# A hybrid decoder step on one core: input projection as seven block products, output projection from float16 parts

## The chip, the cores and the metric

The kernel runs on one core of a Trainium2 chip. The metric is device time in microseconds (us); lower is better. Each core has TensorE (PE, with its weight loads as PEld), VectorE (DVE), ScalarE (ACT), GpSimd (POOL) and SyncE (SP, which here only issues DMAs). Every engine runs its own instructions in program order and waits on semaphores for the others.

## What is computed

Two layers run over 2048 prompt tokens and 64 sample tokens (8 sequences of 8), with a model width of 1024.

```python
h = rmsnorm(x, norm_pre)
p = h @ w_in          # 1024 x 3344, cut into four head groups
# A short gated convolution    (x, b, c, z: 256 columns each)
# B gated linear attention     (q, k, v, z: 256 each, and 16 columns of a low-rank gate)
# C sliding-window attention   (q 256, k 128, v 128, z 256)
# D attention to 256 memory tokens (q, z: 256 each)
x = x + rmsnorm(concat(A, B, C, D) @ w_out, norm_post)
```

All of it is float32. The states and caches of the groups are outputs too.

## The kernel before, in words

The program is a sequence of stages: `start` (norm and transposes of the first 1024 tokens, and the products of the memory tokens), then four passes: layer 0 tokens 0 to 1023, layer 0 tokens 1024 to 2047 with the 64 sample tokens, and the same for layer 1. Each pass is a stage `units` (input projection and head groups) and a stage `out` (output projection, norm, residual, and the transposed h of the next pass).

A float32 product is made of float16 parts. h and the weights are scaled and split into a high and a low part, and a product is high x high, low x high and high x low: three "pieces". h lies transposed in `h_hi` and `h_lo`, 8 blocks of 128 rows (k) by tokens. The input weights are cut into 26 tiles of 128 columns and a narrow one of 16 (the gate, `lr`). For each tile and each step of 512 tokens (in the second passes also spans that take in the sample tokens, of 320 and 256 columns) PE runs 8 k x 3 pieces into one of two PSUM banks that alternate:

```python
        def proj_bank(it):
            return it["inst"] % 2
```

An instance waits until the reader of the one before the last has freed its bank. ACT reads most tiles out of PSUM (L2308, L2304), DVE some of group A (L2511, L2514). Weight tiles live in a ring of four (`w_raw` float32, `w_parts` high and low). In a first pass SP loads them (L1765), POOL scales them in place (L2841), ACT makes the high part (L2281), POOL the low one (L2836), and SP keeps both in DRAM (L1773), from where the second pass loads them (L1759).

Eight units (D0, B0, B1, C0, A0, C1, D1, A1: head group and half) follow each other in a pass. The order of everything in a pass, on all engines, comes from `plan_units`, which lays pieces of projection between the rows of the units' own work by estimated durations. So a wait of one engine holds all that stands behind it.

The output projection (L3011) takes the mixed heads and `w_out` in float32r high and low parts, again three pieces of 8 k, 512 columns each, two halves of the width: 48 matmuls a tile of 128 tokens. It waits for the bank's reader two turns back. In `start`, POOL's only steps in the loop over 8 token tiles are `mean ** -0.5` (the rows of L1283, called pow here), DVE's norm of a tile waits for its pow, and PE transposes the tile.

## Time and profile before

| what | value |
|---|---|
| timed runs, median | 2183.58 us (2179.11, 2183.58, 2184.03) |
| profiled execution | 2180.1 us span, 3.5 us below that median |
| PE busy | 2071.0 us, 95% |
| DVE busy | 1228.0 us, 56% |
| ACT busy | 855.0 us, 39% |
| POOL busy | 335.2 us, 15% |
| unit stages | 48 to 453, 553 to 1015, 1112 to 1525, 1622 to 2074 us |

Busy is the time in which an engine executes; shares are of the span. Matmuls are pipelined, so a busy PE need not be PE at its peak. The time between the stages named is the start and the four output stages.

### The profile page before, as it was taken

The page shows a single profiled execution, that of the slowest core. Times are in us where ns is not written, and L with a number is a line of the kernel's source. Part 1 is how long each engine was busy: PE and PEld are TensorE (multiplying, and loading weights), DVE is VectorE, ACT ScalarE, POOL GpSimd, SP SyncE. Part 2 cuts the span into 40 slices and gives each one's busy share as a digit, 9 for nine tenths or more (in the row PEclk, how much of TensorE's full clock was granted, in tenths as well). Part 3 has the DMA queues.
Part 4 walks back from the last instruction along what each step waited for, and adds up shares of the span by engine and source line. Part 5 has one row for each costly group of instructions (what it writes and reads, how often), then busy time and mean ns, then how long its engine had stood idle before and what let it go on. Part 6 is the DMA issues. An engine that isn't in the chain of part 4 may idle for free. (4 is left out here: it accounts for less than half of the span.)

```text
span 2180.1 us, 43454 instructions
## 1 busy us (share of the span) xinstructions
PE 2071.0 (95%) x16698; PEld 1321.2 (61%) x16698; DVE 1228.0 (56%) x2763; ACT 855.0 (39%) x1981; POOL 335.2 (15%) x267
## 2 busy tenths in 40 slices
PE   8999899999999998997999998999999999999898
PEld 4555455568666665666855444455776666656677
DVE  5477665455367754553645775555644776644423
ACT  4554333444354332333435542343435453232311
POOL 1443332000000000000133342320100000000000
PEclk9999999999999999998999998999999999999999
DMA  7431223347410222335353132223561113131532
GB/s 263 128 98 50 75 72 97 97 154 257 118 48 24 65 61 69 85 101 193 127 137 105 62 84 82 83 89 108 188 237 49 60 41 82 35 94 42 159 123 87
DMA packets 196936, 224.92 MB, mean 103 GB/s; under 512 B 53974, under 2 KB 138460, under 8 KB 196700
## 3 DMA queue, kind: packets, MB, share of 16 engines
q1 hardware_dynamic: 193620, 211.55, 31.3%
q10 hardware_dynamic: 3112, 10.59, 1.5%
q8 instruction: 135, 2.21, 0.4%
q14 instruction: 69, 0.57, 0.1%
HBM read 144.98 MB, written 66.10 MB: 97 GB/s over the span
## 5 line engine op out<-in xcount | busy, mean ns | idle before, releaser
L1934 PE MATMUL bank<-h_hi,w_parts 128*128 128x512 f16 (+4 forms) x4240 | 841.1, 344 | 17.5 <-ACTq L2309 9.8
L1934 PEld LDWEIGHTS bank<-h_hi,w_parts 128*128 128x128 f16 (+1 forms) x4240 | 403.2, 98 | 360.4 <-issue 58.0
L1934 PE MATMUL bank<-h_lo,w_parts 128*128 128x512 f16 (+3 forms) x2160 | 441.3, 343 | 3.4 <-DVEq L2560 1.1
L1934 PEld LDWEIGHTS bank<-h_lo,w_parts 128*128 128x128 f16 (+1 forms) x2160 | 205.4, 98 | 176.6 <-issue 18.9
L3011 PE MATMUL bank<-scr_r,tb_r 128*128 128x512 f32 x768 | 192.3, 409 | 21.5 <-DMA scr_r<-w_out_kept 12.4
L3011 PEld LDWEIGHTS bank<-scr_r,tb_r 128*128 128x128 f32 x768 | 149.4, 197 | 56.0 <-issue 13.0
L2308 ACT ACTIVATE tb<-bank 128x512 f32<-128x512 f32 (+1 forms) x140 | 71.3, 509 | 247.8 <-PE bank L1934 227.4
L2841 POOL TENSOR_SCALAR w_raw<-w_raw 128x1024 f32<-128x1024 f32 x46 | 129.6, 2822 | 80.0 <-DMA w_raw<-in_w_in 79.6
L3078 ACT ACTIVATE junk<-bank 128x512 bf16<-128x512 f32 (+1 forms) x68 | 40.6, 597 | 243.7 <-PE bank L3011 233.4
L2441 ACT ACTIVATE scr<-bank,stat 128x256 f32<-128x256 f32 x256 | 117.4, 470 | 34.0 <-DVE stat L2787 31.2
L2461 ACT ACTIVATE scr<-bank 128x1024 f32<-128x1024 f32 x64 | 65.5, 1023 | 163.7 <-PE bank L2205 163.3
L3011 PE MATMUL bank<-w_hi,tb_r 128*128 128x512 f32 x512 | 128.5, 395 | 0.7 <-DVEq L3159 0.7
L2836 POOL TENSOR_TENSOR w_parts<-w_raw,w_parts 128x1024 f16<-128x1024 f32 x46 | 103.5, 2252 | 165.8 <-ACT w_parts L2281 165.6
L2645 DVE COPY_PREDICATED scr<-level_mask,bank 128x128 f32<-128x128 uint8 (+1 forms) x332 | 116.8, 352 | 11.3
L3011 PEld LDWEIGHTS bank<-w_hi,tb_r 128*128 128x128 f32 x512 | 95.5, 188 | 22.3 <-DVEq L3159 1.2
L2304 ACT ACTIVATE tb<-bank 128x512 f32<-128x512 f32 (+1 forms) x80 | 40.7, 508 | 148.9 <-PE bank L1934 116.0
L2857 POOL TENSOR_TENSOR stat_g<-stat_g,minus_half 128x8 f32<-128x8 f32 (+1 forms) x20 | 29.2, 1462 | 403.5 <-DVE stat_g L2693 403.5
L2801 DVE TENSOR_SCALAR scr<-scr,stat 128x256 f32<-128x256 f32 x264 | 87.5, 393 | 2.5
L2810 DVE TENSOR_TENSOR mix_t<-bank,tb 128x256 f32<-128x256 f32 x64 | 27.1, 424 | 95.6 <-PE bank L2230 94.3
L2546 DVE SCALAR_TENSOR_TENSOR tb<-tb,gate_raw 128x512 f32<-128x512 f32 (+1 forms) x80 | 47.6, 594 | 46.2 <-ACT gate_raw L2305 44.2
L2205 PE MATMUL bank<-ident,scr 128*128 128x128 f32 x512 | 69.4, 278 | 3.6 <-DVE scr L2801 3.3
L2774 DVE SCALAR_TENSOR_TENSOR bank<-bank,win_mask 128x512 f32<-128x512 f32 x64 | 44.8, 699 | 43.6 <-PE bank L2186 40.2
(304 smaller groups left out, 2813.8 us busy)
## 6 DMA issues: line engine op xcount, KB each, us to landing
w_in_kept<-w_parts SPq DMA_DIRECT2D x104, 256.0 KB, 4.3
w_parts<-w_in_kept SPq DMA_DIRECT2D x104, 256.0 KB, 2.9
w_raw<-in_w_in SPq DMA_DIRECT2D x48, 512.0 KB, 4.1
out<-scr SPq DMA_DIRECT2D x32, 512.0 KB, 2.6
scr<-in_x_prompt SPq DMA_DIRECT2D x16, 512.0 KB, 4.3
w_out_kept<-scr_r SPq DMA_DIRECT2D x16, 512.0 KB, 6.3
scr_r<-w_out_kept SPq DMA_DIRECT2D x16, 512.0 KB, 5.9
scr<-out SPq DMA_DIRECT2D x16, 512.0 KB, 4.2
```

What stands on the lines that cost most here:

```text
L1934: m = mm(bank[b][0:m_w, 0:c1 - c0], w[:, k, 0:m_w], h[:, k, c0:c1], start=it["piece"] == 0 and k == 0, stop=it["piece"] == 2 and k == KT - 1)
L2205: m = nc.tensor.transpose(bank[b][:, (2 * h + i) * P:(2 * h + i + 1) * P], p[:, o:o + P], ident[:])
L2308: fn(part_of(s, role, pt), src, ACT.Copy, scale=scale).then_inc(tile_copied, 1)
L2441: m = fn(p[:, 256 * x:256 * x + 256], bank[6 + h][:, 256 * i:256 * i + 256], ACT.Exp, bias=z[:, 4 + x:5 + x], scale=1.0 if unit == "C" els ...
L2461: fn(pt.rearrange("p (b n) -> p b n", b=2), psum[:, 2:4, :], ACT.Copy).then_inc(bank_free[2], 1)
L2546: link(stt(z, z, 1.0, raw_gate(span, pt), ALU.add, ALU.mult))
L2645: m = nc.vector.copy_predicated(a.rearrange("p h (m i r) -> p h m i r", i=2, r=v)[:, :, :, 1, :], mask.to_broadcast([w, 2, w // (2 * v), v ...
L2774: link(stt(at[i], at[i], scale, mask.to_broadcast([P, 2, 256]), ALU.mult, ALU.add))
L2801: m = ts(p[:, n * h:n * h + n], p[:, n * h:n * h + n], z[:, at_inv + h:at_inv + h + 1], None, ALU.mult)
L2836: tt(lo_of(t), w_raw[:, t % RING, :, 0:split_width(t)], hi_of(t), ALU.subtract).then_inc(w_lo_done, 1)
L2841: nc.gpsimd.tensor_scalar(raw, raw, W_UP, None, ALU.mult).then_inc(w_scaled, 1)
L3011: m = nc.tensor.matmul(bank[b].rearrange("p (j n) -> p j n", j=RING), lhs[:, t % 2, k, :], rhs[:, :, k, :], start=j == 0 and k == 0, stop= ...
```

## The change

**Input projection.** Tokens, k and weight columns are each cut in two halves: a step's 512 tokens into 256 and 256 (a second pass's with 32 sample tokens each: 288), k into two times four blocks, and two weight tiles of 128 columns make a "duo". A duo and a step are a 2 x 2 product of blocks, and it is computed by seven block products ("visits") in place of eight, from sums of blocks (S1 to S4 of the weights, T1 to T4 of h). A visit is 3 pieces x 4 k = 12 matmuls of 256 columns for each duo. Where a unit has two duos (A, B, C0) and there are no sample tokens, both lie side by side in a bank and share a visit: four weight tiles at once. There are 13 duos. The two banks still alternate, now by visits; only three visits start with an empty bank, the others accumulate on what stands in it after its reader has read it.

**Readers.** ACT reads the visits `s1`, `c11` and the gate; DVE reads the other five, adding the earlier part. Tanh of z and A's products run from SBUF afterwards.

**Weights.** Each layer has 34 blocks of preparation (two for a duo, eight for `w_out`), in first passes only: SP loads, ACT scales and makes the high part of three source blocks, POOL the low part (`prep_sum`, also the four sums), ACT the high part of the sums and the fourth block (`prep_split`), POOL their low part (`prep_low`), SP keeps both (`w_kept`) and loads the duo into a ring of two (`w_ring`). There is one buffer for high and one for low parts. Layer 0 has 2 blocks prepared in `start`, layer 1 has 6 in the output stage before it.

**h.** Where h is transposed, DVE, ACT and POOL also make T1 to T4 with their high and low parts (`h_low_sums`, `h_high_rest`, `h_low_rest`); the units wait for the last (`hx_ready`).

**Output projection.** The parts are float16 in place of float32r; its counts and shapes stay, and `w_out`'s parts are loaded in eight blocks.

```diff
-RING = 4
+HK = KT // 2
...
+VISITS = [(A11, B11, "s1"), (S2, T2, "u2"), (A12, B21, "c11"), (S3, T3, "u3"), (S1, T1, "c22"), (A22, T4, "c21"), (S4, B22, "c12")]
+FRESH = ("s1", "u2", "c22")
+LAND_ON = dict(c11=(0, 0), u2=(0, 1), c12=(0, 1), c21=(1, 0), u3=(1, 1), c22=(1, 1))
...
+ON_ACT = ("s1", "c11", "lr")
...
+    def prep_scale(act, link, k):
+
+        fn = nc.scalar.activation
+        act.wait_ge(p_in[k % 2], landed_by(k))
+        link(fn(p_raw[:, k % 2], p_raw[:, k % 2], ACT.Copy, scale=W_UP))
+        if k > 0:
+            act.wait_ge(kept_hi, 16 * k)
+            act.wait_ge(p_low_done, k)
+        if is_sub(k):
+            fn(p_hi[:, 0:3], p_raw[:, k % 2, 1:4], ACT.Copy).then_inc(p_hi_done, 1)
...
+    def prep_sum(pool, link, k):
+
+        tt = nc.gpsimd.tensor_tensor
+        a21, a11, a22, a12 = (p_raw[:, k % 2, i] for i in range(4))
+        pool.wait_ge(p_hi_done, k + 1)
+        if k > 0:
+            pool.wait_ge(kept_lo, 16 * k)
+        link(tt(p_lo[:, 0:3], p_raw[:, k % 2, 1:4], p_hi[:, 0:3], ALU.subtract))
+        link(tt(a22, a21, a22, ALU.add))
+        link(tt(a21, a11, a21, ALU.subtract))
+        link(tt(a11, a22, a11, ALU.subtract))
+        tt(a12, a12, a11, ALU.subtract).then_inc(p_sum_done, 1)
...
+    EARLY_PREPS = (2, 6)
...
             for t in range(tiles):
                 z = st_first[:, t]
                 pool.wait_ge(mean_done, t + 1)
                 nc.gpsimd.tensor_tensor(z[:, 3:4], z[:, 2:3], minus_half[:], ALU.pow).then_inc(root_done, 1)
+                if t == 2:
+                    prep_sum(pool, link, 0)
+                if t == 3:
+                    prep_low(pool, 0)
+                if t == 5:
+                    prep_sum(pool, link, 1)
+                for u, half in {3: [(1, 0)], 4: [(1, 1)], 5: [(3, 0)], 6: [(3, 1)], 7: [(5, 0)]}.get(t, ()):
+                    h_low_rest(pool, u, half)
+                if t == 6:
+                    prep_low(pool, 1)
+            lr_low(pool, build[0])
+            h_low_rest(pool, 5, 1)
+            for half in range(2):
+                h_low_rest(pool, 7, half)
+            pool.drain().then_inc(hx_ready, 1)
             pool.drain().then_inc(closed["pool"], 1)
...
+                    if it["no"] == 0 and v["use"] > 0:
+                        pe.wait_ge(bank_free[b], v["use"])
...
+                        if j == 0 and v["first"]:
+                            pe.wait_ge(ring_in[load_no[(d, w)] % 8], 16 * (1 + load_no[(d, w)] // 8))
+                        for k in range(HK):
+                            m = mm(bank[b][:, n * x:n * x + n], w_ring[:, d % 2, w, int(j == 2), k, :],
+                                   (hb_lo if j == 1 else hb_hi)[:, v["h"], k, tok],
+                                   start=v["name"] in FRESH and it["no"] == 0 and k == 0, stop=j == 2 and k == HK - 1, skip_group_check=True)
...
-                            m = nc.tensor.matmul(bank[b].rearrange("p (j n) -> p j n", j=RING), lhs[:, t % 2, k, :], rhs[:, :, k, :],
+                            if t == 0 and j < 2 and k % HK == 0:
+                                pe.wait_ge(wo_in[4 * n + 2 * (j == 1) + k // HK], 16)
+                            m = nc.tensor.matmul(bank[b], lhs[:, t % 2, k, :], rhs[:, k, :],
```

The order of instructions changes with it, at three places that matter below. POOL in `start`, before (`stat` holds the mean of a tile; the line of pow is 1283; the memsets prepare the units):

```order
L1278 MEMSET minus_half 128x1
L1283 ISA
L1283 TENSOR_TENSOR stat<-stat,minus_half 128x1 x8
L2822 MEMSET low 1x1088
L2825 MEMSET gla_state 128x256
L2826 MEMSET k_prev 128x256
L2827 MEMSET v_prev 128x128
```

After (line 1573 is pow, 1326 to 1330 `prep_sum`, 1342 `prep_low`, 1455 `h_low_rest`, with `hb_lo` the low parts of h's blocks):

```order
L1455 TENSOR_TENSOR hb_lo<-ring_f,hb_hi 128x8x128
L1573 TENSOR_TENSOR stat<-stat,minus_half 128x1
L1455 TENSOR_TENSOR hb_lo<-ring_f,hb_hi 128x8x128
L1573 TENSOR_TENSOR stat<-stat,minus_half 128x1
L1326 TENSOR_TENSOR p_lo<-p_raw,p_hi 128x768
L1327 TENSOR_TENSOR p_raw<-p_raw 128x256
L1328 TENSOR_TENSOR p_raw<-p_raw 128x256
L1329 TENSOR_TENSOR p_raw<-p_raw 128x256
L1330 TENSOR_TENSOR p_raw<-p_raw 128x256
L1455 TENSOR_TENSOR hb_lo<-ring_f,hb_hi 128x8x128
L1573 TENSOR_TENSOR stat<-stat,minus_half 128x1
L1455 TENSOR_TENSOR hb_lo<-ring_f,hb_hi 128x8x128
```

The fragment starts behind the fourth pow: between it and the last one POOL now has the sums of a second weight block, and low parts of h; before, the eight pows followed each other.

PE where unit B0's projection begins, before (line 1934 is the projection, 2230 and 2181 D0's attention, 1981 the gate):

```order
L1934 MATMUL bank<-h_hi,w_parts 128x512 x12
L2230 MATMUL bank<-scr,mem_v 64x128 x8
L1934 MATMUL bank<-h_lo,w_parts 128x512 x8
L1981 MATMUL bank<-low,gate_w 128x512
L1934 MATMUL bank<-h_hi,w_parts 128x512 x12
L2181 MATMUL bank<-mem_kt,tb 128x256 x4
L1934 MATMUL bank<-h_hi,w_parts 128x512 x4
L1934 MATMUL bank<-h_lo,w_parts 128x512 x8
```

After (2253 is the projection, 2550 and 2501 D0's attention, 2525 transposes, 2301 the gate):

```order
L2253 MATMUL bank<-hb_hi,w_ring 128x256 x4
L2501 MATMUL bank<-mem_kt,tb 128x256 x4
L2525 MATMUL bank<-ident,scr 128x128 x8
L2253 MATMUL bank<-hb_hi,w_ring 128x256 x4
L2253 MATMUL bank<-hb_lo,w_ring 128x256 x8
L2253 MATMUL bank<-hb_hi,w_ring 128x256 x16
L2253 MATMUL bank<-hb_lo,w_ring 128x256 x8
L2253 MATMUL bank<-hb_hi,w_ring 128x256 x16
```

A tile's k loop in groups of 512 columns has become visits of 4 k by piece and duo; the row of `hb_hi,w_ring` behind `ident,scr` belongs to B0's second duo, whose weights are the last to arrive.

SP behind the start's layer loads, before (`w_raw` is a tile's load, `w_in_kept` its store):

```order
L1765 DMA w_raw<-in_w_in 128x8x128 x4
L1773 DMA w_in_kept<-w_parts 128x8x32
L1773 DMA w_in_kept<-w_parts 128x1024 x4
L1765 DMA w_raw<-in_w_in 128x8x128 x3
L1773 DMA w_in_kept<-w_parts 128x1024 x8
```

After (`p_raw` is a block's load, `w_kept` its stores, high and low, `w_ring` a load of the ring):

```order
L1299 DMA p_raw<-in_w_in 128x2x128 x8
L1365 DMA w_kept<-p_hi 128x7x256
L1365 DMA w_kept<-p_lo 128x7x256
L1299 DMA p_raw<-in_w_in 128x2x128 x4
L1365 DMA w_kept<-p_hi 128x7x256
L1365 DMA w_kept<-p_lo 128x7x256
L1299 DMA p_raw<-in_w_in 128x2x128 x4
L1376 DMA w_ring<-w_kept 128x1024 x7
L1365 DMA w_kept<-p_hi 128x7x256
L1365 DMA w_kept<-p_lo 128x7x256
L1299 DMA p_raw<-in_w_in 128x2x128 x4
```

A block's loads and its two stores now follow each other in one queue, with the ring's loads between them.

## Rows read from the trace of the kernel before

**Rows 1.** Head of the page and its part 1: busy time of each engine.
```profile
span 2180.1 us, 43454 instructions
PE 2071.0 (95%) x16698; PEld 1321.2 (61%) x16698; DVE 1228.0 (56%) x2763; ACT 855.0 (39%) x1981; POOL 335.2 (15%) x267
```

**Rows 2.** Windows: span, busy us (instructions) by engine, granted clock, DMA; start, and four unit stages.
```profile
0.00:48.00 48.00, 41.51 (x159) 22.28 (x160) 26.98 (x40) 24.83 (x43) 6.53 (x17) 1.00 0.83 281
...
sum 1732.00, PE 1640.68 PEld 982.01 DVE 1003.70 ACT 691.22 POOL 297.88; mean PE 410.17 PEld 245.50 DVE 250.93 ACT 172.80 POOL 74.47
```

**Rows 3.** Timeline of PE: start, duration in us, line, operation, count; three places.
```profile
54.90 3.62 PE L1934 MATMUL bank<-h_hi,w_parts 128*128 128x512 f16 x16
58.35 0.81 PE L1934 MATMUL bank<-h_lo,w_parts 128*128 128x512 f16 x3
...
582.22 1.04 PE L1934 MATMUL bank<-h_hi,w_parts 128*128 128x256 f16 x8
583.09 1.04 PE L1934 MATMUL bank<-h_lo,w_parts 128*128 128x256 f16 x8
...
2104.74 2.00 PE L3011 MATMUL bank<-w_hi,tb_r 128*128 128x512 f32 x8
2106.58 0.61 PE L3011 MATMUL bank<-w_lo,tb_r 128*128 128x512 f32 x2
```

**Rows 4.** Page part 5, then the groups by form: busy us, mean ns of one.
```profile
L1934 PE MATMUL bank<-h_hi,w_parts 128*128 128x512 f16 (+4 forms) x4240 | 841.1, 344 | 17.5 <-ACTq L2309 9.8
L1934 PE MATMUL bank<-h_lo,w_parts 128*128 128x512 f16 (+3 forms) x2160 | 441.3, 343 | 3.4 <-DVEq L2560 1.1
...
L1934 PE MATMUL bank<-h_hi,w_parts 128*128 128x512 f16 x2496 | 594.1, 383 | 12.2 <-ACTq L2309 9.2 <-issue 2.1
L1934 PE MATMUL bank<-h_hi,w_parts 128*128 128x256 f16 x832 | 110.6, 275 | 1.0 <-issue 0.5
```

**Rows 5.** Timeline of the start: POOL, then PE.
```profile
37.50 0.55 POOL L1283 TENSOR_TENSOR stat<-stat,minus_half 128x1 f32<-128x1 f32 x1 [3.76 <-DVE stat L1371]
...
47.89 1.89 PE L1934 MATMUL bank<-h_hi,w_parts 128*32 128x512 f16 x8 [0.36 <-issue]
```

**Rows 6.** Instructions by tile, w_raw and w_parts: ns minimum/median/maximum, first and last start.
```profile
L2841 POOL TENSOR_SCALAR w_raw<-w_raw x46: 2762/2772/3210, 63.1 to 1431.1; 128x1024 f32<-128x1024 f32 x46
...
L2281 ACT ACTIVATE w_parts<-w_raw x46: 1040/1057/1058, 69.9 to 1461.0; 128x1024 f16<-128x1024 f32 x46
L2836 POOL TENSOR_TENSOR w_parts<-w_raw,w_parts x46: 2120/2137/2902, 74.1 to 1462.3; 128x1024 f16<-128x1024 f32 x46
```

**Rows 7.** DMA issues: KB each, median us from issue to landing.
```profile
w_in_kept<-w_parts SPq DMA_DIRECT2D x104, 256.0 KB, 4.3
```

**Rows 8.** Timeline of SP's queue behind the start.
```profile
50.64 0.39 SPq L1799 DMA_DIRECT2D scr<-out  x1
...
58.87 2.23 SPq L1765 DMA_DIRECT2D w_raw<-in_w_in  x3
```

**Rows 9.** Groups by form: a read of PSUM with a tile on DVE.
```profile
L2514 DVE SCALAR_TENSOR_TENSOR tb<-bank,tb 128x512 f32<-128x512 f32 x12 | 8.2, 687 | 5.7 <-PE bank L1934 5.7
...
L2514 DVE SCALAR_TENSOR_TENSOR tb<-bank,tb 128x256 f32<-128x256 f32 x8 | 3.4, 422 | 1.2 <-PE bank L1934 1.2
```

**Rows 10.** Windows: four stretches of linear attention summed; all work, then line 1934 alone.
```profile
sum 639.00, PE 605.66 PEld 371.49 DVE 461.70 ACT 282.02 POOL 142.91; mean PE 151.42 PEld 92.87 DVE 115.43 ACT 70.50 POOL 35.73
...
sum 639.00, PE 438.07 PEld 219.48; mean PE 109.52 PEld 54.87
```

**Rows 11.** Timeline of two places: DVE alone, and DVE beside POOL.
```profile
69.16 1.37 DVE L2801 TENSOR_SCALAR scr<-scr,stat 128x256 f32<-128x256 f32 x4
...
1140.68 5.35 DVE L2801 TENSOR_SCALAR scr<-scr,stat 128x256 f32<-128x256 f32 x4
1141.33 4.29 POOL L2836 TENSOR_TENSOR w_parts<-w_raw,w_parts 128x1024 f16<-128x1024 f32 x2
```

**Rows 12.** Waits before line 1934's instructions: us, times, by releaser.
```profile
  ACTq L2309: 9.8, 6
```

1478 lines of the change are left out of this document (828 added, 650 removed).

## Prediction

> **What bounds the kernel now.** I read the page first: TensorE (PE) is busy 2071.0 of the 2180.1 us span, VectorE (DVE) 1228.0, ScalarE (ACT) 855.0, GpSimd (POOL) 335.2 [rows 1]. Then busy time by stage: the four unit stages, 1732 us, hold the input projection, and there PE works 1640.7 us, DVE 1003.7 [rows 2]. So PE bounds the kernel on average and the sum starts with PE's work. But the change puts work on DVE and POOL, so I also read single stretches: how PE's matmuls follow each other, the start, the stretches where DVE is fullest. The profiled span is 2180.1; the runs' median is 2183.58, so I add 3.5 to a span to forecast a time.
>
> **The price of a matmul.** In a row without idle time, 16 matmuls of 512 columns start at 54.90 and the next begin at 58.35: 215.6 ns each. Eight of 256 columns go from 582.22 to 583.09: 108.8 ns [rows 3]. The two give 0.417 ns a column and 2.0 ns a matmul, almost no fixed price.
>
> **1. Input projection, -125 us.** Counted in the order of instructions: before 6400 matmuls with 2,703,360 columns (3840 of 512, 1280 of 320, 1280 of 256), after 9056 with 2,390,784 (6792 of 256, 2264 of 288). Before: 6400 x 2.0 ns + 2,703,360 x 0.417 ns = 1140 us. After: 9056 x 2.0 + 2,390,784 x 0.417 = 1015. Seven eighths of the columns, less a little since the narrow gate tile costs more.
>
> **2. Output projection, -23 us.** 1600 matmuls of 512 columns become float16. Eight float32r ones go from 2104.74 to 2106.58, 230 ns each [rows 3]; at 215.6 that saves 1600 x 14.4 ns = 23 us. The output stages are nearly all PE, so I count it whole. Together -148.
>
> **3. The start, +30 (14 to 38).** Now the first projection matmul stands at 47.89 [rows 5]. The change puts the sums and low parts of two weight blocks and the low parts of h's sums on POOL, in program order between the eight root steps (pow) that DVE's norms wait for, and the units wait for the last of them. Neither operation is in the trace of before; by the nearest rows, a 128x1024 difference is 2137 ns on POOL [rows 6] (so 768 columns 1.6 us), and a pow is 0.55 [rows 5]. For a 256-column sum I take 0.65, between a quarter of 2137 and some overhead. A block then costs 1.6 + 4 x 0.65 = 4.2 us for its sums and 2.14 for its low part; eight h parts cost 17.1. That is 30 us of POOL work, where POOL was busy 6.53 of 48 [rows 2]. Least: POOL is full from about 28.6 (when ScalarE has the first block ready) and ends at 62, +14. But the steps are in a ring: a pow waits for a norm on DVE, which stands behind h sums that wait for POOL's low parts of the pair before. Walked in order, the fourth pow comes at 33 (the last stood at 37.50 [rows 5]), the seventh near 58, the eighth near 69, and the last low part at 78 to 82. I take 78: +30.
>
> **4. Feeding the first units, +30 (10 to 40).** After the start SP first issues the layer's loads (8.2 us between 50.64 and 58.87 [rows 8]), then the next weight blocks. One block's chain is serial, since there is one buffer for high and one for low parts: sums 4.2, split on ACT 1.05, low part 2.14 [rows 6], and the store's landing, 4.3 for 256 KB [rows 7] (here 458 KB, so if anything more): 11.7 us. The first of these loads is issued 11 us after the start's last row, as now (47.89 to 58.87), and lands some 4 later, as that of [rows 7] transfer does, near 93; ScalarE's scaling and high parts take 1.8, so block 5 is kept near 93 + 1.8 + 4 x 11.7 = 142 and in the ring some 3 later, a load like those, near 145. B0's two weight pairs share a visit, so its first rows need blocks 2 to 5. PE has, before it, the gate tile (80 x 108.8 ns = 8.7), D0's projection (84 x 2 x 108.8 ns = 18.3) and a few attention rows: 36 us after 78, so it stands from 114 to about 144. Layer 1 has six blocks prepared in the output stage before, and no such gap. Later a pair costs 23.4 us of feeding against about 29 of PE's time (the first unit stage's 405 us, 48 to 453, over 13 pairs, less 125/52 saved): it keeps ahead, though narrowly.
>
> **5. VectorE where it is fullest, +28 (0 to 60).** DVE now adds five of seven visits: about 256 operations of 128x256 and 132 of 512 columns, by the nearest row 422 and 687 ns [rows 9]: 108 + 91 = 199 us. In the four stretches of the gated linear attention (639 us) PE works 605.7, of it 438.1 on the projection, and DVE 461.7, 72% [rows 10]; that is 34% of the projection's 841.1 + 441.3 us [rows 4]. So 34% of the gain (43 us) should come there, and 34% of DVE's new work (68 us) goes there, plus some 10 of contention: 540 us of DVE in 596. At 91% an engine that works in order is late for much of what PE waits for. Nothing of the gain lost is one end, all of it and some new stalls the other; I take two thirds, 28.
> On contention: four operations that took 1.37 us at 69.16 took 5.35 at 1140.68, when two POOL differences ran beside them [rows 11]. The Trainium skill ("SBUF — State Buffer", section "Who interferes with whom") says that VectorE shares a pair of ports with GpSimd and that whoever has it locks the other out; the rows agree. POOL gives up 46 scalings and 46 differences (226 us [rows 6]) and takes on 52 sums of blocks at 4.2, 68 low parts of blocks and 32 of h at 2.14 (432), all but the last in first passes and the stages before them.
>
> **6. Heads of queues in the first passes, +15 (0 to 40); second output stage, +2.** About 60 blocks put on ACT two steps that wait for the store of the block before, in front of bank evictions. Now PE waits 9.8 us in all for ACT's part of the bank turns [rows 12]. If one in four of 60 comes 1 us late and PE feels it, that is 15. The borders from output to units cost nothing: 10 us of remaining output matmuls cover the last h parts.
>
> **Sum.** -148 + 30 + 30 + 28 + 15 + 2 = -43: a span of 2137, a time of 2140.
>
> **Rivals.** *A: the start and the feeding are hidden.* If SP's early loads and POOL are quicker than walked, only terms 5 and little else remain: -148 + 28 + 10 = -110, a time of 2074. For it: POOL is busy only 15% of the span [rows 1]. Against: it works strictly in order among the pows, and the least of term 3 is already +14. Chance 0.22.
> *B: bank turns decide, and the kernel does not gain.* Two PSUM banks alternate as before, but are turned 518 times instead of 270, a visit of 84/7 = 12 matmuls of 256 columns being 1.3 us where two tiles are not side by side. An ACT or DVE reader that comes late by more than the other bank's visit stops PE. Each 0.1 us that a turn waits on average costs 52 us, so 0.08 us beyond the sum above ends the gain, and 0.15 gives 2220. For it: DVE readers in order, 687 ns each, behind long operations. Against: PE now waits only some 10 us for evictions at 270 turns [rows 12]. Chance 0.18, of which 0.05 within 0.3% of no change.
> *C: a matmul has a price of its own.* The busy rows read 594.1 us for 2496 matmuls of 512 columns and 110.6 for 832 of 256 [rows 4], 238 and 133 ns, which is 28 ns fixed and 0.41 a column. Then term 1 is 9056 x 28 ns + 2,390,784 x 0.41 ns less the same of before, -54 instead of -125: a time of 2211. Against: these rows count the tail of each group and stretches at a lower clock; the spacings of rows 3 do not show it. Chance 0.05.
> The Trainium skill ("TensorE: Matmul & The Clock Gate", section "Back-to-back issue gap") gives 131 ns for 512 columns and 81 for 128 in a steady stream, so that many small matmuls cost more than few large; by that rule the projection would gain nothing and lose over 100 us. The trace's 215.6 ns at 512 columns disagrees with it.
>
> **How the numbers follow.** My forecast, some of each of terms 3 to 6, holds from 2100 to 2177 with a chance of 0.55; A lies below, B and C from 2177 up. About 0.3%, 6.6 us, is what a measurement can tell from no change. Faster: 0.55 + 0.22 = 0.77; the same: 0.05 of B; slower: 0.13 + 0.05 = 0.18. The range from 2065 to 2195 leaves out the lower third of A, 0.07, and of B and C 0.13.
>
> **What would show it.** Right: first projection row near 80 us; a PE gap of some 30 us before B0's second row of projection at 110 to 145, absent in layer 1; 256-column rows spaced at 109 ns; output tiles of 48 x 215.6 = 10.35 us; DVE about 1450 us busy (1228 + 199 and the sums of h), POOL about 540 (335 - 226 + 432); DVE near 90% in the stretches of the linear attention. Wrong: PE waits for bank evictions by 50 us or more, spread over all passes, most on DVE (B); 256-column rows at 130 ns (C); first row below 65 us (A); or PE waiting for the ring late in a first pass, where I hold that the feeding keeps ahead.

## The result, and the profile after

The changed kernel takes 2525.39 us (median of 4 runs, 2520.49 to 2526.51), against 2182.72 us before beside them: 1.157 times as long, with a 95% interval of [1.1555, 1.1587]. The prediction was 2140. The forecast of faster was wrong, and the time lies 330 us above its range.

The head and part 1 of the page, with the slices of PE's granted clock in tenths (compare [rows 1]):

```profile
span 2523.9 us, 50652 instructions
PE 2050.5 (81%) x19354; PEld 1498.1 (59%) x19354; DVE 1479.7 (59%) x3279; ACT 965.2 (38%) x2047; POOL 575.1 (23%) x541
...
PEclk8878889969999989898988997899799998989799
```

DVE and POOL have about the work that was forecast (1450 and 540). But PE, 95% busy before, is busy for 81% of a longer span, and in 18 of 40 slices the granted clock is under nine tenths. So PE has no more work than before; it stands more, and more of its work runs at the lower clock.

Windows of the kernel after, cut at the first projection row and the first output row of each stage: the start, then units and output of layer 0's two passes and the units of layer 1's first (columns: stretch, length, busy us and instructions of PE, PEld, DVE, ACT and POOL, granted clock, DMA share, GB/s):

```profile
0.00:87.60 87.60, 53.48 (x158) 27.36 (x158) 42.12 (x56) 36.04 (x55) 36.54 (x34) 0.85 0.58 193
87.60:604.40 516.80, 388.80 (x4100) 315.64 (x4101) 289.14 (x601) 217.60 (x404) 200.35 (x172) 0.86 0.51 150
604.40:718.30 113.90, 95.79 (x457) 46.34 (x458) 76.00 (x107) 47.80 (x102) 26.88 (x26) 0.94 0.34 117
718.30:1208.80 490.50, 419.62 (x4595) 330.37 (x4596) 297.42 (x830) 160.73 (x414) 20.99 (x32) 0.92 0.29 83
1208.80:1343.90 135.10, 107.11 (x481) 50.30 (x482) 74.81 (x99) 66.44 (x121) 69.34 (x61) 0.90 0.57 179
1343.90:1823.20 479.30, 379.78 (x4100) 310.48 (x4101) 290.30 (x604) 206.68 (x395) 168.19 (x149) 0.88 0.50 152
```

The same cut of the kernel before, for the units and outputs of layer 0's two passes:

```profile
47.90:453.20 405.30, 382.61 (x3116) 200.83 (x3116) 241.53 (x538) 170.20 (x354) 126.66 (x62) 0.98 0.30 88
453.20:552.80 99.60, 99.26 (x456) 80.92 (x457) 55.59 (x83) 40.93 (x93) 8.82 (x16) 0.97 0.65 227
552.80:1003.90 451.10, 429.46 (x4250) 284.01 (x4251) 253.22 (x678) 170.83 (x452) 20.93 (x32) 0.99 0.26 77
1003.90:1112.30 108.40, 105.53 (x480) 85.92 (x481) 57.03 (x85) 42.46 (x95) 8.79 (x16) 0.98 0.43 144
```

The first unit stage is 111.5 us longer with PE's busy time nearly the same (388.8 against 382.6); the second, which prepares no weights, is 39.4 us longer. The stages against the terms of the sum, in us of the span:

| part | forecast | measured |
|---|---|---|
| start (term 3) | +30 | +39.7 |
| four unit stages (terms 1, 4, 5, 6) | -125 + 30 + 28 + 15 = -52 | +111.5, +39.4, +71.2, +38.1 = +260.2 |
| four output stages (term 2 and +2) | -21 | +14.2, +26.7, +11.3, -8.3 = +43.9 |
| sum | -43 | +343.8 |

Where the unit stages' time is can be read from PE's timeline. First the price of a matmul, from rows without idle time (start, duration, line, operation, count; in brackets the idle time before and its releaser):

```profile
94.94 1.04 PE L2253 MATMUL bank<-hb_hi,w_ring 128*128 128x256 f16 x8
95.81 0.60 PE L2253 MATMUL bank<-hb_lo,w_ring 128*128 128x256 f16 x4
...
105.08 1.92 PE L2253 MATMUL bank<-hb_hi,w_ring 128*128 128x256 f16 x8
106.79 1.06 PE L2253 MATMUL bank<-hb_lo,w_ring 128*128 128x256 f16 x4
...
139.48 1.04 PE L2253 MATMUL bank<-hb_hi,w_ring 128*128 128x256 f16 x4
157.46 2.08 PE L2501 MATMUL bank<-mem_kt,tb 64*128 64x256 f32 x8 [16.95 <-ACTq L2751]
...
500.99 0.61 PE L2253 MATMUL bank<-hb_hi,w_ring 128*128 128x256 f16 x4 [1.05 <-DVE tb L2808]
515.39 1.04 PE L2253 MATMUL bank<-hb_hi,w_ring 128*128 128x256 f16 x4 [13.79 <-DMA w_ring<-w_kept]
...
530.48 1.04 PE L2253 MATMUL bank<-hb_hi,w_ring 128*128 128x256 f16 x8
554.01 1.89 PE L2253 MATMUL bank<-hb_hi,w_ring 128*128 128x256 f16 x8 [22.50 <-ACT tb L2615]
```

Eight matmuls take 0.87 us from 94.94 to 95.81, 109 ns each as forecast: the price of the columns was right. From 105.08 to 106.79 they take 1.71, 214 ns: here the granted clock is 0.50, the lower of its two levels (1.2 in place of 2.4 GHz), behind a wait of 3.93 us at 103.40. Then three stands of one stage: 16.95 us for ACT's scores, 13.79 us for weights that are not yet in the ring, 22.50 us for ACT's read of a bank.

What ACT does in these stands (its timeline, the rows of the weight preparation alone; L1310 scales a block, L1315 and L1317 make high parts of an input block and of a `w_out` block, L1335 the high part of the sums):

```profile
141.44 1.06 ACT L1335 ACTIVATE p_hi<-p_raw 128x1024 f16<-128x1024 f32 x1 [2.30 <-POOL p_raw L1330]
142.40 1.04 ACT L1310 ACTIVATE p_raw<-p_raw 128x1024 f32<-128x1024 f32 x1
145.59 0.84 ACT L1315 ACTIVATE p_hi<-p_raw 128x768 f16<-128x768 f32 x1 [2.15 <-DMA w_kept<-p_hi]
152.90 1.06 ACT L1335 ACTIVATE p_hi<-p_raw 128x1024 f16<-128x1024 f32 x1 [6.47 <-POOL p_raw L1330]
...
540.24 1.06 ACT L1310 ACTIVATE p_raw<-p_raw 128x1024 f32<-128x1024 f32 x1 [2.63 <-DMA p_raw<-in_w_out]
541.32 1.06 ACT L1317 ACTIVATE p_hi<-p_raw 128x1024 f16<-128x1024 f32 x1
544.69 1.06 ACT L1310 ACTIVATE p_raw<-p_raw 128x1024 f32<-128x1024 f32 x1 [2.31 <-DMA p_raw<-in_w_out]
545.78 1.06 ACT L1317 ACTIVATE p_hi<-p_raw 128x1024 f16<-128x1024 f32 x1
```

The steps of one block wait for POOL's sums, and for the store of the block before; ACT's bank reads and scores (L2751) stand in its queue behind them. From 540 ACT goes through `w_out`'s blocks at 4.45 us each, half of it waiting for a block's load, while PE stands for the bank that ACT has still to read.

In the second passes no weights are prepared, and the stands are of another kind. PE, second pass of layer 1, in the linear attention:

```profile
2112.02 1.04 PE L2253 MATMUL bank<-hb_hi,w_ring 128*128 128x256 f16 x8
...
2116.65 0.44 PE L2394 MATMUL bank<-scr 128*64 128x128 f32 x4 [1.25 <-DVEq L2985]
...
2120.11 0.69 PE L2394 MATMUL bank<-scr 128*64 128x128 f32 x4 [1.63 <-DVEq L2985]
...
2123.55 0.48 PE L2389 MATMUL bank<-scr 128*64 128x64 f32 x4 [2.11 <-DVEq L2985]
...
2125.99 1.87 PE L2413 MATMUL bank<-heads_one,mix_t 128*128 128x2 f32 x8 [1.11 <-ACT mix_t L2705]
2131.46 1.09 PE L2425 MATMUL bank<-ident,mix_t 128*128 128x128 f32 x4 [3.59 <-DVE mix_t L3003]
2135.06 1.89 PE L2253 MATMUL bank<-hb_hi,w_ring 128*128 128x256 f16 x8 [2.52 <-DVE tb L2808]
```

From 2112.02 to 2135.06 no projection row stands between the head group's own rows, and every stand of over 1 us among these ends with a step of DVE or ACT. Stretches of more than 5 us from the start of one projection row to the start of the next were 2, 1, 2 and 1 in the four unit stages before (14.6, 7.5, 15.5 and 7.3 us); after they are 10, 6, 7 and 6 (124.4, 85.8, 109.5 and 84.5 us). PE's idle time in all (span less busy time) rises from 109 to 473 us, and the time at the lower clock from 96 to 492 us.

Projection rows wait themselves, too, and mostly for the reader of their bank (the largest of PE's waits before L2253 in the whole trace: us in total, times, longest):

```profile
PE bank L2253 <- DVE tb L2808: 61.3, 38, 5.8
PE bank L2253 <- ACT tb L2615: 40.8, 7, 22.5
PE bank L2253 <- DVE spare L2808: 22.6, 19, 2.6
PE bank L2253 <- DMA w_ring<-w_kept: 18.3, 7, 13.8
```

Added up over the four unit stages, PE's waits for readers of projection banks rise from 13 to 134 us (54, 20, 40 and 20 by stage; 90 of them on DVE), its waits before the head groups' rows from 49 to 203, and those for weights in the ring from nothing to 18.

### The profile page after: what moved, and what is told of

Same layout as the page of the kernel before. It is cut to its first block and busy times, and to the rows that moved or that the text cites. A ratio compares the mean times of both kernels' runs of the same rounds, so it can differ in the third digit from the quotient of the medians.

```text
span 2523.9 us, 50652 instructions
## 1 busy us (share of the span) xinstructions
PE 2050.5 (81%) x19354; PEld 1498.1 (59%) x19354; DVE 1479.7 (59%) x3279; ACT 965.2 (38%) x2047; POOL 575.1 (23%) x541
## 5 line engine op out<-in xcount | busy, mean ns | idle before, releaser
L2253 PE MATMUL bank<-hb_hi,w_ring 128*128 128x256 f16 (+1 forms) x5824 | 808.0, 284 | 161.4 <-DVE tb L2808 61.3
L2253 PEld LDWEIGHTS bank<-hb_hi,w_ring 128*128 128x128 f16 x5824 | 566.5, 100 | 303.4 <-DVE tb L2808 73.5
L2253 PE MATMUL bank<-hb_lo,w_ring 128*128 128x256 f16 (+1 forms) x2912 | 436.2, 284 | 1.1
L3311 PE MATMUL bank<-scr_h,tb_h 128*128 128x512 f16 x1536 | 350.4, 390 | 27.4 <-DVEq L3442 25.5
L2253 PEld LDWEIGHTS bank<-hb_lo,w_ring 128*128 128x128 f16 x2912 | 288.5, 101 | 64.7 <-issue 15.1
L3311 PEld LDWEIGHTS bank<-scr_h,tb_h 128*128 128x128 f16 x1536 | 152.7, 100 | 215.4 <-DVEq L3442 28.1
L2808 DVE SCALAR_TENSOR_TENSOR tb<-bank,s 128x256 f32<-128x256 f32 (+1 forms) x218 | 112.8, 517 | 151.6 <-PE bank L2253 128.6
L1326 POOL TENSOR_TENSOR p_lo<-p_raw,p_hi 128x768 f16<-128x768 f32 x52 | 89.2, 1716 | 294.3 <-ACT p_hi L1315 223.4
L1342 POOL TENSOR_TENSOR p_lo<-p_raw,p_hi 128x1024 f16<-128x1024 f32 x52 | 113.9, 2191 | 90.8 <-ACT p_hi L1335 90.6
L2747 ACT ACTIVATE scr<-bank,stat 128x256 f32<-128x256 f32 x256 | 117.3, 470 | 38.1 <-DVE stat L3090 34.9
L2808 DVE SCALAR_TENSOR_TENSOR tb<-bank,tb 128x256 f32<-128x256 f32 (+1 forms) x146 | 76.0, 521 | 87.2 <-PE bank L2253 82.3
L3152 POOL TENSOR_TENSOR stat_g<-stat_g,minus_half 128x8 f32<-128x8 f32 (+1 forms) x20 | 29.1, 1455 | 389.2 <-DVE stat_g L2993 389.2
L1310 ACT ACTIVATE p_raw<-p_raw 128x1024 f32<-128x1024 f32 x68 | 71.5, 1052 | 48.7 <-DMA p_raw<-in_w_out 17.3
L2615 ACT ACTIVATE tb<-bank 128x256 f32<-128x256 f32 (+1 forms) x74 | 34.6, 468 | 129.5 <-PE bank L2253 87.6
```

What stands on the lines that cost most here:

```text
L1310: link(fn(p_raw[:, k % 2], p_raw[:, k % 2], ACT.Copy, scale=W_UP))
L1326: link(tt(p_lo[:, 0:3], p_raw[:, k % 2, 1:4], p_hi[:, 0:3], ALU.subtract))
L1342: tt(p_lo[:, 3:7], p_raw[:, k % 2], p_hi[:, 3:7], ALU.subtract).then_inc(p_low_done, 1)
L2253: m = mm(bank[b][:, n * x:n * x + n], w_ring[:, d % 2, w, int(j == 2), k, :], (hb_lo if j == 1 else hb_hi)[:, v["h"], k, tok], start=v["na ...
L2747: m = fn(p[:, 256 * x:256 * x + 256], bank[6 + h][:, 256 * i:256 * i + 256], ACT.Exp, bias=z[:, 4 + x:5 + x], scale=1.0 if unit == "C" els ...
L2808: m = stt(dst, seen(bank[b], o0, o1, form), UNSCALE, other, ALU.mult, ALU.add)
```

## The experiments

Names used below. **W**: the feeding of weights (the chain of the preparation, and what waits behind it). **D**: VectorE, in order, is late (term 5). **B**: the bank's turns (rival B). **R**: where the planner puts the projection rows. **S**: in the unit stages the head groups' own chain over DVE, ACT and PE sets the time, and the projection's columns partly fill its waits, so that columns removed are not time. All runs: median, ratio to before with its interval, stage lengths in the profiled execution (u: units, o: output), time at the lower clock, in us. The kernel before was run again beside each, with medians from 2181.55 to 2185.73, so a difference of some 4 us between two medians of this table says nothing.

| kernel | median | ratio | start | u1 | o1 | u2 | o2 | u3 | o3 | u4 | o4 | low clock |
|---|---|---|---|---|---|---|---|---|---|---|---|---|
| before | 2182.72 | 1 | 47.9 | 405.3 | 99.6 | 451.1 | 108.4 | 408.1 | 102.4 | 451.8 | 105.4 | 96 |
| after | 2525.39 | 1.157 [1.156, 1.159] | 87.6 | 516.8 | 113.8 | 490.5 | 135.1 | 479.3 | 113.7 | 489.9 | 97.1 | 492 |
| out_f16_before | 2155.97 | 0.987 [0.985, 0.989] | 49.0 | 406.8 | 96.5 | 449.1 | 105.1 | 409.2 | 95.2 | 448.4 | 98.9 | 101 |
| fine_off_before | 2177.08 | 0.996 [0.995, 0.997] | 49.0 | 404.1 | 99.4 | 451.5 | 110.1 | 404.7 | 101.2 | 451.7 | 105.2 | 89 |
| fine_off_after | 2479.66 | 1.136 [1.133, 1.138] | 87.3 | 504.1 | 115.8 | 479.8 | 136.6 | 468.9 | 116.0 | 477.0 | 97.2 | 451 |
| no_feed_l1 | 2449.27 | 1.121 [1.119, 1.124] | 87.2 | 519.8 | 113.9 | 490.6 | 122.6 | 413.9 | 116.0 | 490.6 | 97.1 | 431 |
| start_rest_dve | 2519.14 | 1.153 [1.151, 1.156] | 80.3 | 520.2 | 113.9 | 490.2 | 133.6 | 475.5 | 115.6 | 490.1 | 97.1 | 482 |
| prep_split_pool | 2548.44 | 1.166 [1.164, 1.169] | 86.4 | 525.0 | 115.9 | 491.3 | 135.9 | 492.1 | 113.6 | 489.8 | 97.1 | 513 |
| prep_one_sum | 2490.69 | 1.140 [1.138, 1.141] | 82.9 | 495.0 | 115.7 | 491.0 | 132.0 | 471.9 | 113.8 | 490.0 | 97.1 | 472 |
| early_two_l1 | 2563.63 | 1.174 [1.171, 1.176] | 87.4 | 514.3 | 113.7 | 490.5 | 128.2 | 523.9 | 113.6 | 493.3 | 97.1 | 526 |
| unshared | 2515.52 | 1.151 [1.149, 1.153] | 88.1 | 535.5 | 109.2 | 476.0 | 136.2 | 489.0 | 110.6 | 476.1 | 97.1 | 417 |
| readers_act | 2514.50 | 1.152 [1.150, 1.154] | 88.2 | 537.4 | 114.2 | 471.1 | 135.2 | 483.5 | 115.5 | 470.5 | 97.1 | 510 |
| both_off | 2421.50 | 1.110 [1.106, 1.113] | 87.6 | 539.4 | 111.8 | 472.0 | 123.7 | 404.6 | 115.5 | 468.7 | 97.1 | 440 |
| late_rows | 2564.52 | 1.173 [1.171, 1.176] | 87.6 | 526.0 | 116.0 | 497.2 | 136.2 | 494.8 | 114.3 | 495.3 | 97.1 | 538 |
| ahead_one_before | 2185.68 | 1.001 [1.000, 1.002] | 49.4 | 407.9 | 99.3 | 452.9 | 108.4 | 410.9 | 101.6 | 452.5 | 105.0 | 107 |
| seven_eighths_before | 2102.76 | 0.963 [0.961, 0.966] | 49.7 | 388.5 | 99.7 | 426.3 | 108.4 | 396.1 | 99.7 | 423.8 | 104.7 | 124 |
| padded_after | 2540.83 | 1.163 [1.161, 1.165] | 87.2 | 520.1 | 115.9 | 501.1 | 128.8 | 472.1 | 113.7 | 503.4 | 97.1 | 373 |
| four_off | 2392.84 | 1.097 [1.095, 1.099] | 87.1 | 538.1 | 110.5 | 466.4 | 119.0 | 401.3 | 109.0 | 465.6 | 97.0 | 368 |

### First: the terms of the sum

**out_f16_before**, the output projection's parts in float16 in the kernel before:

```diff
-    w_parts, w_hi = twice(ctx, "w_parts", F16, "w_hi", F32R, [P, RING, KT, P], [P, RING, 2, KT, P])
+    w_parts, w_hi = twice(ctx, "w_parts", F16, "w_hi", F16, [P, RING, 2, KT, P])
...
-    scr, scr_r = twice(ctx, "scr", F32, "scr_r", F32R, [P, SCRATCH])
+    scr, scr_r = twice(ctx, "scr", F32, "scr_r", F16, [P, 2 * SCRATCH], [P, SCRATCH])
```

> The kernel before with the output projection's parts in float16 in place of float32r and nothing else changed, the order of instructions and the count of matmuls being the same. The prediction's term 2: each of 1600 matmuls of 512 columns takes 215.6 ns in place of 230, 23 us in all, and since the output stages are TensorE's nearly throughout the time falls by 15 to 25 us, to about 2160; narrower loads and stores of the parts may add a little. The rival: the output stages are set by the chain of norm and transposes between tiles and the time stays within 7 us.

It saves 29.7 us (1.3%), more than the 15 to 25 expected, with no price elsewhere. The matmuls of the output projection follow each other at 216 ns in place of 231 (medians at the full clock), which is some 24 us; PE's waits for the loads of `w_out`'s parts fall from 12.4 to 6.9 us besides. Term 2 was right in kind and a little small, and this version beats both kernels.

**fine_off_after** and **fine_off_before** leave out 264 of DVE's 332 masked copies in the linear attention, the same in both kernels:

```diff
-                    for j, (n, v) in enumerate(fine_of(s)):
+                    for j, (n, v) in list(enumerate(fine_of(s)))[-1:]:
```

> The changed kernel with the same 264 masked copies left out, 93 us of VectorE work. Theory D: the kernel stands at 2525 and falls by at least half of the work taken away, 45 to 110 us (a wait less also keeps TensorE's clock up), in all four unit stages alike, much more than the kernel before falls. Theory W: VectorE's lateness is not what is paid; 0 to 20 us, as in the kernel before.

> The kernel before with 264 of the 332 masked copies on VectorE left out (of the gated linear attention's fine levels only the last is copied, so its scores lack the others); nothing else changes, the order of instructions least of all. They are 264/332 of 116.8 us, some 93 us of VectorE work, 23 us a unit stage. Theory D (since the change VectorE is late and what it costs comes out of the time; before, TensorE bounded): 0 to 15 us faster, since TensorE waited for VectorE only in single places. Theory W (what costs the time is the preparation of the weights in the first passes): the same here, 0 to 15. It is the base for the next run.

DVE's busy time falls by 87.7 us before and by 85.2 after; that is worth 8.6 us before and 46 us after, 10 to 13 in each unit stage. So about half of this work stands on the path of the changed kernel, and a tenth of it did before. The 46 us are the low end of what D was expected to give, and little of what was lost (344 us): D is a part and not the whole.

**no_feed_l1**, layer 1 without its weight preparation; it takes layer 0's kept blocks:

```diff
+        k = min(k, PREPS - 1)
...
-        sp.dma_start(w_ring[:, d % 2, w], w_kept[l, d, w]).then_inc(ring_in[n % 8], 16)
+        sp.dma_start(w_ring[:, d % 2, w], w_kept[0, d, w]).then_inc(ring_in[n % 8], 16)
...
-        plan = plan_units(second, [] if second else range(early, PREPS * (l + 1)))
+        plan = plan_units(second, [] if second or l else range(early, PREPS * (l + 1)))
```

> The changed kernel in which layer 1 takes the weights that layer 0 prepared (so layer 1 computes with layer 0's matrices), and so prepares none in its own output stage before and first pass; the planner orders that pass anew. Everything else stays. Theory W (the preparation's steps on ScalarE and GpSimd stand before bank readers and hold them up): the third unit stage, 479 us now against 408 before the change, falls by 35 to 60 us to what the second passes show (about 40 above the kernel before less their sample rows), the output stage before it by some 15; time 2455 to 2480. Theory D (VectorE late, in all passes): the third unit stage falls by less than 15 us, time about 2505. The other stages are the same by both.

76 us less: 65.4 in the first unit stage of layer 1 and 12.5 in the output stage before it, under 4 in any other. The window of that unit stage:

```profile
1334.10:1748.00 413.90, 365.39 (x4101) 303.80 (x4102) 254.41 (x604) 133.91 (x319) 13.45 (x21) 0.93 0.28 85
```

With POOL at 13 us of work in place of 168, and ACT at 134 in place of 207, this stage is still longer than before (408.1), with about 30 us less of columns in it: some 35 us above what the columns alone would give. So W is real, and something else is left. DVE's 604 instructions of this stage take 254.4 us here, 290.3 in the changed kernel: beside POOL's preparation the same work takes DVE 36 us longer. This is a part of what the preparation costs, and no run separates it from the waits.

### Second: what in the feeding costs

**start_rest_dve** makes h's low parts of the start on DVE in place of POOL, **prep_split_pool** moves ACT's second step of a block, the high part of the sums, to POOL (ACT is then never held by POOL's sums), **prep_one_sum** leaves out three of the four sums of a block:

```diff
-                for u, half in {3: [(1, 0)], 4: [(1, 1)], 5: [(3, 0)], 6: [(3, 1)], 7: [(5, 0)]}.get(t, ()):
-                    h_low_rest(pool, u, half)
...
+                if t % 2:
+                    for half in range(2):
+                        h_low_rest(dve, t, half, tt)
+            dve.drain().then_inc(hx_ready, 1)
```

```diff
+        pool.wait_ge(p_sum_done, subs_by(k))
+        nc.gpsimd.tensor_copy(p_hi[:, 3:7], p_raw[:, k % 2]).then_inc(p_hs_done, 1)
...
-        nc.scalar.activation(p_hi[:, 3:7], p_raw[:, k % 2], ACT.Copy).then_inc(p_hs_done, 1)
+        pass
```

```diff
-        link(tt(a22, a21, a22, ALU.add))
-        link(tt(a21, a11, a21, ALU.subtract))
-        link(tt(a11, a22, a11, ALU.subtract))
```

> The changed kernel with the 8 low parts of h's sums in the start made on VectorE behind its own norms, in place of GpSimd; all the rest stays, the weight blocks' work on GpSimd too. The first projection matmul now stands at 87.6 us (47.9 before the change). Prediction's term 3 (the ring: a pow waits for a norm, the norm for h sums, these for GpSimd's low parts): GpSimd loses 17 us of work, VectorE gains some 10, and the first projection comes 15 to 30 us earlier, the time falling by as much at most, to about 2500; some of it may be lost again at the next wait for weights, since these come no earlier. The rival: the weights' landing and ScalarE set the start, and the first projection moves by less than 5 us.

> The changed kernel with the high part of a block's sums (128x1024 on ScalarE, 1.05 us, 52 times) made on GpSimd right behind the sums, so that ScalarE has no step left that waits for GpSimd's sums; GpSimd's own chain grows by some 2 us a block. Two sides of theory W. W1, the heads of ScalarE's queue: PE's waits behind ScalarE go (the trace shows ScalarE standing 35 us for those sums in the first unit stage and 11 in the third) and both first passes fall, together 20 to 60 us, time 2465 to 2505. W2, the serial chain of a block is what the first passes are short of: it grows by 2 us on 52 blocks, and the first unit stages grow by 20 to 60 us, time 2545 to 2585.

> The changed kernel with three of the four sums of a weight block left out on GpSimd (so the sums of blocks of the weights are wrong), each about 0.78 us, 2.3 us of a block's chain, 52 times; the order of instructions stays. Theory W in either form: the first unit stages, 517 and 479 us, fall by 15 to 50 us and 8 to 30 us, since the sums stand in the chain and before ScalarE's head; the start and the output stage before layer 1 fall by 2 to 8; time 2440 to 2500. If GpSimd's work is not what the preparation costs (but ScalarE's own three steps, or the stores), under 10 us in all.

The start falls by only 7.3 us when POOL is relieved of h (and the time by 6, at the edge of the noise), between the 15 to 30 that the ring of term 3 was to give and the rival's under 5; by 4.7 with fewer sums. Taking the step off ACT's queue made the kernel slower, by 23 us. That is what was expected if the chain of a block grows by 2 us (W2), but it did not grow. Two rows of one block in prep_split_pool, and its busy times:

```profile
118.98 1.65 POOL L1326 TENSOR_TENSOR p_lo<-p_raw,p_hi 128x768 f16<-128x768 f32 x1 [8.96 <-ACT p_hi L1315]
125.02 2.13 POOL L1343 TENSOR_TENSOR p_lo<-p_raw,p_hi 128x1024 f16<-128x1024 f32 x1
...
PE 2055.5 (81%) x19354; PEld 1501.0 (59%) x19354; DVE 1519.8 (60%) x3279; ACT 913.2 (36%) x1995; POOL 631.7 (25%) x593
```

From the first sum to the end of the low part this takes 8.2 us, and in the changed kernel 8.1 (136.55 to 144.69); the medians of the 52 blocks are 8.8 and 9.2. What grew is DVE's busy time, by 40 us with the same 3279 instructions: 21 in the first unit stage and 17 in the third, which are 8.2 and 12.8 us longer, none in the second, which is 0.8 us longer. So the slowdown goes with POOL's added work beside DVE, and the gain that W1 expected of a freer ACT did not come. Cutting about 2.3 us of POOL's work from each block gave 35 us back, 21.8 of it in the first unit stage. That run makes the chain shorter and relieves DVE (9 us less in each of these stages), so which of the two pays isn't shown.

**early_two_l1** prepares two blocks of layer 1 ahead in place of six:

```diff
-    EARLY_PREPS = (2, 6)
+    EARLY_PREPS = (2, 2)
```

> The changed kernel with two weight blocks of layer 1 prepared in the output stage before it in place of six, as in layer 0. Theory W with prediction's term 4 (TensorE stands for B0's second duo when only two blocks are ahead): the third unit stage grows by 20 to 40 us from 479 to the first's 517, the output stage before it (135) falls by 5 to 12; time 2535 to 2555. The rival: the first stage is slow for other reasons (the layer's first loads, the start's state of the queues), and the third grows by less than 10 us.

The output stage before gets 6.9 us shorter, the unit stage 44.6 us longer, a little more than expected: 523.9, near layer 0's 516.8. Layer 0's first stage is longer than layer 1's for the four blocks fewer that it has ahead.

### Third: turns, readers, order

**unshared** gives each duo its own visits (728 turns of the bank in place of 518); **readers_act** gives ACT all the reads of PSUM, as copies (DVE's additions are left out); **both_off** is that with no_feed_l1:

```diff
-        together = [duos] if len(group) == 1 else [[d] for d in duos]
+        together = [[d] for d in duos]
```

```diff
-ON_ACT = ("s1", "c11", "lr")
+ON_ACT = ("s1", "u2", "c11", "u3", "c22", "c21", "c12", "lr")
...
```

> The changed kernel in which two duos never share a visit: 728 visits in place of 518, same matmuls and columns; 132 VectorE reads of 512 columns become 264 of 256 (some 21 us more VectorE work), ScalarE's likewise; the planner orders anew. The prediction's rival B (what a bank turn costs): each of the 210 more turns costs 0.1 to 0.3 us, 20 to 60 us and more in the first passes than in the second; time 2545 to 2590. Theory D alone (VectorE's work at about half its price, as shown by the copies left out): about 10 us, 2535. If neither, within 7 us of 2525, or faster since smaller visits give the planner finer pieces.

> The changed kernel with all seven visits read out of PSUM by plain copies on ScalarE; VectorE's additions of the earlier parts are left out (so five of seven block products never meet and the projection is wrong), same visits, turns and matmuls; the planner orders anew. VectorE loses about 195 us of work and ends near what it had before the change (1228), ScalarE gains about 190. Theory D: what the second passes lost (490 us against 451 before, where 33 less were due) comes mostly from VectorE, and each falls by 30 to 60 us, all four unit stages together by 120 to 220; time 2310 to 2405. The rival (bank turns and the order, whoever reads): under 15 us a stage, time above 2465.

> The same with layer 1 taking layer 0's prepared weights as well (no preparation in its first pass): both suspected costs away in the third unit stage. If D and W are all there is, that stage comes to what TensorE's columns alone give, 408 less 30, 375 to 390 us; with W alone away it was 414. If a third cause is left (the clock, the turns, ScalarE now), it stays above 395. The whole at 65 to 85 us below the run without the additions.

With 210 more turns the kernel is 10 us faster: 14 less in each second pass, 10 to 19 more in the first. So a turn has no fixed price of the kind that was expected here for B (0.08 us each would be +17). But PE's waits for readers of projection banks did rise, from 134 to 171 us, while its waits before the head groups' rows fell from 203 to 153: the planner had ordered all anew. Without DVE's reads and additions (194 us of DVE's work less) the second passes are 19.4 us shorter, which is neither D's 30 to 60 nor the rival's under 15; the first passes are longer, where ACT now has both the reads and the weights (in the first, PE's waits for the ring rise from 17 to 69 us). The two edits together leave the third unit stage at 404.6, some 26 us above what the columns alone would give, and the second passes at 472.0 and 468.7, above before (451): a cause beside W and D remains.

**late_rows** orders the visits so that ACT's second read comes later and two visits stay in one buffer; **ahead_one_before** lets the planner of the kernel before hold projection rows one bank turn back in place of two:

```diff
-VISITS = [(A11, B11, "s1"), (S2, T2, "u2"), (A12, B21, "c11"), (S3, T3, "u3"), (S1, T1, "c22"), (A22, T4, "c21"), (S4, B22, "c12")]
+VISITS = [(A11, B11, "s1"), (S2, T2, "u2"), (S3, T3, "u3"), (A12, B21, "c11"), (S1, T1, "c22"), (A22, T4, "c21"), (S4, B22, "c12")]
...
```

```diff
-        p = pieces[0] if pieces and (pieces[0]["inst"] < 2 or pieces[0]["inst"] - 2 in freed) else None
+        p = pieces[0] if pieces and (pieces[0]["inst"] < 1 or pieces[0]["inst"] - 1 in freed) else None
```

> The changed kernel in which the two visits u2 and u3 are read into the small buffer s1 in place of the rows of the unit's tiles, and come before c11; so three visits in place of one are read without a free row, and two more may stand finished in the banks (five of seven in place of three may run ahead of the rows). Same matmuls, columns, visits and reads, their forms nearly the same; the parts no longer add up, so the projection is wrong. Theory R (a row of a unit's tiles is held until the unit before has read it; the projection that may run ahead of it shrank from two tiles, 48 matmuls of 512 columns, 10.3 us, to three visits, 36 of 256, 3.9 us, or 7.8 where two duos share; so stretches of the head groups' own rows stand without projection between, TensorE waits in them and its clock falls): the stretches of over 5 us without projection in a second pass (6, 85 us) fall by a third or more, the second passes from 490 to 445 to 475 us, the time to 2400 to 2480. Theory D (VectorE's work, which is the same) and the clock by itself: no stage changes by more than 7 us, time 2510 to 2540.

> The kernel before in which the planner lets the projection run one tile and span ahead of the rows in place of two (24 matmuls of 512 columns, 5.2 us, in place of 10.3); nothing else is changed: same instructions on every engine, in another order. Theory R: stretches without projection appear as in the changed kernel (before: 1 of 7.5 us in a second pass), TensorE waits in them; each unit stage grows by 10 to 50 us, time 2225 to 2380. If the look-ahead doesn't matter, under 7 us a stage, time below 2205.

The stretches without projection rows in the second unit stage fell from 85 to 62 us, and the stage got 6.7 us longer; the whole is 39 us slower, which neither side expected. The order of the kernel before can be made that much stricter at no cost (+0.1%). R is not borne out: shorter stretches did not give time.

### Fourth: what are columns worth

**seven_eighths_before** leaves out columns of the third piece in the kernel before, 142 us of them by their price, and adds nothing; **padded_after** does two of four k of the third piece twice in the changed kernel, 163 us more of columns (the planner knows, and orders anew); **four_off** is no_feed_l1, readers_act, unshared and fine_off_after together:

```diff
-                    for k in range(k0, k1):
+                    ks = range(KT - 1, KT) if it["piece"] == 2 and k0 > 0 else range(k0, k1)
+                    for k in ks:
```

```diff
-                        for k in range(HK):
+                        for k in ([0, 1] if j == 2 else []) + list(range(HK)):
...
```

> The kernel before with 3 of the 24 matmuls of each tile and span left out (three k of the high-by-low piece, so the low part of the weights is only partly used), 810 of 6400 matmuls and 337,920 columns, one eighth, 142 us by the spacing of rows 3; nothing else is changed, the order of instructions least of all. So it is what the change promised without anything that it added. The prediction's term 1 (TensorE bounds the unit stages, columns taken away are time): 100 to 142 us faster, time 2040 to 2085. Theory S (the head groups' own chain from VectorE and ScalarE to TensorE and back is nearly as long as the stage; the projection is what fills its waits, and with less of it TensorE stands there and its clock falls): much of it stays as waiting; 20 to 80 us faster, time 2105 to 2165, TensorE's idle time and the time at the lower clock well above the kernel before.

> The changed kernel with 14 matmuls for 12 in each visit and duo (two k of the high-by-low piece are added twice, so the product is wrong), 1456 matmuls more, 163 us by the spacing at the full clock; the planner knows the length, and orders anew; reads, visits and all else as they are. If TensorE's columns bound the changed kernel: 130 to 163 us slower, time 2655 to 2690. Theory S and W (waits bound it, which the added work fills, and a busier TensorE keeps its clock): 20 to 90 us slower, time 2545 to 2615, with less waiting and less time at the lower clock.

> Four edits of before in one on the changed kernel: layer 1 takes layer 0's prepared weights, all visits are read by plain copies on ScalarE, two duos never share a visit, and 264 masked copies of VectorE are left out. The projection and the attention are wrong. Alone, readers on ScalarE, unshared visits and the copies took 20, 14 and 12 us off a second pass (490). If these are parts of one cost that add up (VectorE and the long reads in the head groups' chains), the second passes come to 440 to 452 and the third stage, 405 with two of the edits, to 385 to 398; so the kernel before (451, 408) is reached or passed. If they overlap, the second passes stay at 458 to 470: then the head groups' chain itself, with a projection cut into halves of a duo, is what stays.

Even in the kernel before, with nothing added, 142 us of columns are worth 83 us, 58%; that lies between what was expected of S (up to 80) and of term 1 (from 100), next to S. In the changed kernel 163 us more of them cost 15.5 us, a tenth, less than either side expected. Page and second unit stage of padded_after:

```profile
PE 2178.3 (86%) x20810; PEld 1618.6 (64%) x20810; DVE 1486.1 (59%) x3279; ACT 964.9 (38%) x2047; POOL 573.2 (23%) x541
...
723.20:1224.30 501.10, 453.04 (x4959) 360.76 (x4960) 298.11 (x830) 160.24 (x414) 20.98 (x32) 0.95 0.30 86
```

PE works 33.4 us more in this stage (453.04 against 419.62) in a stage only 10.6 us longer, and the granted clock rises from 0.92 to 0.95. The changed kernel isn't bound by PE's columns; they lie in its waits. This is what S says of the columns. That the head groups' chain by itself sets the time isn't shown: no run changes that chain alone but fine_off_after. Nor do the reliefs add up. The three of four_off that touch the second unit stage (no_feed_l1 doesn't) had given it 19.4, 14.5 and 10.7 us, 45 if they added, and together they give 24.1, so they lie in part on the same waits. It stays at 466.4, 15 above before and 48 above what the columns alone would give (451.1 - 33).

## Why the prediction was wrong, point by point

**The steps that failed: "So PE bounds the kernel on average and the sum starts with PE's work", and with it term 1 counted at full price; and in term 4 "it keeps ahead, though narrowly".** Between the forecast of -43 and the measured +344 lie 387 us. The feeding has 135 of them over the 45 of terms 4 and 6 (in part by estimate, below), the start 10, the output stages without the six blocks of weights 52. The other 190 are the unit stages without their feeding: forecast at -97 (terms 1 and 5), measured at +92. The -125 us of columns were there: counted over the trace, the projection at its full-clock price falls from 275.6 to 246.2 us in the first unit stage and from 294.2 to 261.2 in the second. But a busy share of 95% does not say that all of it bounds. PE's rows in a unit stage are of two kinds, the head groups' rows, which wait in turn for DVE and ACT, and the projection's, which fill these waits. Take fillers away, and waits are left: in seven_eighths_before 42% of the columns' time was not gained, and PE's idle time rose from 109 to 155 us, before a single operation was added. At that rate term 1 is some 52 us too large, an estimate from another kernel than the changed one; the rest of the 190 is in the next points only in part.

**Term 4 and term 6, the feeding, 45 forecast, about 180 measured.** 65.4 + 12.5 us in layer 1 (no_feed_l1), and for layer 0 an estimate of 103, its first unit stage less the 413.9 that layer 1's takes without feeding. The serial chain of a block was right where it runs alone: POOL begins blocks at 136.55 and 148.02, 11.5 us apart where I worked out 11.7, with larger sums and a shorter landing. The stand at 140 to 157 lies where term 4 had one, but by luck: term 4 had 30 us of waiting for the ring, and PE stands 17 us for ACT's scores, which are held behind ACT's wait for POOL's sums. That is term 6's mechanism, sized there at 15 us in all. What failed in term 4 is "it keeps ahead, though narrowly": the blocks of this stage follow each other at 17.3 us (398.2 us over 23 steps), not 11.7. ACT and POOL take their steps of a block in an order shared with the units; prep_one_sum, with 2.3 us less in each block, still has 16.5:

```profile
L1326 POOL TENSOR_TENSOR p_lo<-p_raw,p_hi x24: 1637/1642/2492, 103.2 to 501.4; 128x768 f16<-128x768 f32 x24
```

This is the tile view of the first operation of each block in the first unit stage (ns minimum, median, maximum, then the first and the last start). PE stands for the ring at 515 and behind `w_out`'s blocks at 554. PE waiting for the ring late in a first pass was named as a sign of being wrong. And layer 1 is not free of it, as I had it; six blocks ahead save 44.6 us there, not all. A part of these 180 us is DVE, slower beside POOL: 36 us of its busy time in layer 1's first unit stage (no_feed_l1), where term 5 had 10 us for contention in all.

**Term 5, VectorE, 28 in a range of 0 to 60.** DVE's additional work was sized right: readers_act takes 194 us of it off (1479.7 to 1285.6), where 199 was forecast. It gives 19.4 in each second pass, 39 in the two, above the 28 but inside the range; the first passes can't be read, since ACT takes the reads over. DVE "near 90%" did not come: from the first to the last masked copy of the linear attention it is busy for 80% in a first pass (120.8 of 150.7 us; before 102.4 of 132.2). The second passes lost some 72 us each against the columns (39.4 + 33 in the first), so most of it is not this additional work.

**What the sum left out: the clock.** In the kernel before, 96 us ran at the lower clock, in the changed one 492. An estimate of the price: 277 and 1614 matmuls began in such stretches, and by the median spacings of their shapes at the two levels they took some 27 and 117 us longer, so about 90 us of PE's time (not tested alone, and not all of it on the path) come from standing first and being slow afterwards. The Trainium skill ("TensorE: Matmul & The Clock Gate", section "HAM oscillation — how this bites in real kernels") counts half of the time at the lower clock as lost; by that the estimate would be 198 us here. The rows give less, since PE is busy for only 287 of these 492 us. padded_after shows the same from the other side: more work for PE, and 119 us less at the lower clock.

**Term 3, the start, +30 forecast, +39.7 measured.** DVE and POOL in the start of the changed kernel (L1573 pow, L1455 low parts of h, L1678 norm):

```profile
33.18 0.55 POOL L1573 TENSOR_TENSOR stat<-stat,minus_half 128x1 f32<-128x1 f32 x1
33.77 1.28 DVE L1678 SCALAR_TENSOR_TENSOR mix_t<-mix_t,stat,scr 128x1024 f32<-128x1024 f32 x1 [9.03 <-POOL stat L1573]
...
39.61 2.12 POOL L1455 TENSOR_TENSOR hb_lo<-ring_f,hb_hi 128x1024 f16<-128x1024 f32 x1
39.67 3.14 DVE L1678 SCALAR_TENSOR_TENSOR mix_t<-mix_t,stat,scr 128x1024 f32<-128x1024 f32 x1 [3.36 <-POOL stat L1573]
...
59.83 0.55 POOL L1573 TENSOR_TENSOR stat<-stat,minus_half 128x1 f32<-128x1 f32 x1
...
72.17 0.55 POOL L1573 TENSOR_TENSOR stat<-stat,minus_half 128x1 f32<-128x1 f32 x1
...
83.09 4.24 POOL L1455 TENSOR_TENSOR hb_lo<-ring_f,hb_hi 128x1024 f16<-128x1024 f32 x2 [4.83 <-ACT hb_hi L1447]
87.64 1.87 PE L2245 MATMUL bank<-hb_hi,w_lr 128*32 128x256 f16 x8 [7.17 <-POOLq L1588]
```

The steps came nearly as walked: the fourth pow at 33, the seventh at 60 (58 forecast), the eighth at 72 (69); the last low part ended at 87 in place of 78 to 82. The reason was less right than the times: with POOL's low parts of h taken out of the ring (start_rest_dve) the eighth pow still comes at 67.6 and the start is only 7.3 us shorter. In both runs that pow stands behind POOL's wait of 7.6 and 7.8 us for ACT's high part of the second block. Rival A falls with the first projection row at 87.6.

**Term 2 and the output stages, -21 forecast, +43.9 measured.** Float16 alone gave its 29.7 us; in the changed kernel it comes through in the last output stage only (-8.3), where no next h is made. In the others the sums of h are new work: DVE 76.0 us in place of 55.6 in the first. PE's longest waits in the output stage before layer 1:

```profile
PE bank L3311 <- DVEq L3442: 18.4, 4, 11.9
PE bank L3327 <- DVE rot L3405: 7.2, 2, 5.4
```

"The borders cost nothing" looked at the border and not at the stage, in which output matmuls (L3311) now wait until DVE has freed their bank: 25.5 us in the four stages, 0.7 before. 12.5 us of the stage before layer 1 are the six blocks of weights; that the rest is h's sums is read from these waits and not tested.

**Rivals.** B's sign came: PE waits 134 us for readers of projection banks, in all four passes, 90 of them on DVE, where "50 us or more, spread over all passes, most on DVE" was to show it. So B's mechanism, a reader that comes late and stops PE, is a part of the loss. Its count by turns isn't: 210 more turns raised these waits by some 36 us and the kernel got faster all the same (unshared). No run gives the projection another bank, or its readers a place further ahead, so what B costs in time stays open. C is refuted by the 109 ns. That the removed work had been filling waits was not among the rivals.

**What stays open.** Of the 48 us that a second unit stage still lacks with four edits undone I can't say how they divide among the head groups' own steps, the clock, the remaining readers and the planner's order. In layer 0's first stage the feeding is an estimate; it was taken away in layer 1 alone.

## What to carry to other kernels

Before counting removed work at its full price, ask what stands between the rows that are removed: where an engine's other rows each wait for another engine, its busy work is filling, and what a column is worth is found by leaving some out and by adding some. A producer chain through four queues that are shared with the main work does not run at its own pace (17.3 us a block here, for a chain of 11.5): its steps wait for their turn in each queue, and everything behind them waits too. The part of this change that shortens each of its matmuls and adds nothing, float16 in the output projection, is the one to keep.

## What the runs showed of the hardware

- A norm of 128x1024 on DVE took 1.28 us alone (33.77) and 3.14 us (39.67) beside a POOL operation of 2.12 us that began 0.06 us before it: longer by nearly the whole of it. The Trainium skill ("SBUF — State Buffer", section "Who interferes with whom") says that the two share a pair of ports under an exclusive lock; the rows agree.
- More work on PE gave a better granted clock: 0.95 in place of 0.92 in the second unit stage of padded_after.
- Matmuls of 512 columns in the output projection followed each other at 216 ns from float16 parts (out_f16_before) and at 231 from float32r ones (before), medians at the full clock; [rows 3] gave 215.6 and 230.
- The same 604 DVE instructions of a first unit stage took 290.3 us beside 168.2 us of POOL's work and 254.4 us beside 13.5 (no_feed_l1).
